# A gated feed-forward layer in split fp32: high-weight products cut into 362, 362 and 364 columns over three PSUM banks in place of four of 272

## The reference, cut to what matters

```python
def _swiglu(x, w_gate, w_up, w_down):
    return (jax.nn.silu(x @ w_gate) * (x @ w_up)) @ w_down

def _layer(x, state, p):
    f = _swiglu(_rmsnorm(x, p['ffn1_norm_pre']), p['ffn1_w_gate'], p['ffn1_w_up'], p['ffn1_w_down'])
    x = x + (0.5 * _rmsnorm(f, p['ffn1_norm_post'])).astype(x.dtype)
    m, new_state = _token_mixer(_rmsnorm(x, p['mix_norm_pre']), *state, p)
    x = x + _rmsnorm(m, p['mix_norm_post']).astype(x.dtype)
    f = _swiglu(_rmsnorm(x, p['ffn2_norm_pre']), p['ffn2_w_gate'], p['ffn2_w_up'], p['ffn2_w_down'])
    x = x + (0.5 * _rmsnorm(f, p['ffn2_norm_post'])).astype(x.dtype)
    return x, new_state
```

## Time and profile before

| | us |
|---|---|
| median of three runs | 3801.59 |
| lowest and highest | 3799.52, 3802.06 |
| the profiled execution, its own time | 3801.82 |
| its span, first to last instruction | 3799.8 |
| mean granted TensorE clock of the span | 0.932 |

### The profile page before, as it was taken

The page is one execution under the profiler, slowest core; times in us unless marked ns, Lnnn a source line. Parts: engine busy times, 40 slices in busy tenths (PEclk is TensorE's granted clock), DMA queues, the critical chain, the costliest instruction groups (busy, mean ns, idle before and its releaser), DMA issues. The chain is left out here.

```text
span 3799.8 us, 68663 instructions
## 1 busy us (share of the span) xinstructions
PE 3450.5 (91%) x25494; PEld 3262.0 (86%) x25494; DVE 1306.9 (34%) x1895; ACT 745.7 (20%) x1228; POOL 1556.6 (41%) x948
## 2 busy tenths in 40 slices
PE   8999899887877998999899998998778789989997
PEld 7999799866747997999889997998667479979997
DVE  2220275366444222221022202763564442132201
ACT  2110222223103112110021102322231021121100
POOL 4555466200004653555445553662000046535553
PEclk9999999999758999999999999999996589999999
DMA  3222122000103231222132222220001122312221
GB/s 120 88 85 84 55 90 86 28 0 0 63 23 100 88 93 56 86 88 84 51 93 88 87 83 61 84 88 20 0 0 63 57 75 88 92 56 88 87 83 64
DMA packets 77404, 258.82 MB, mean 68 GB/s; under 512 B 8272, under 2 KB 10064, under 8 KB 76496
## 3 DMA queue, kind: packets, MB, share of 16 engines
q1 hardware_dynamic: 76976, 256.43, 22.0%
q10 hardware_dynamic: 288, 0.49, 0.0%
HBM read 242.31 MB, written 14.58 MB: 68 GB/s over the span
## 5 line engine op out<-in xcount | busy, mean ns | idle before, releaser
L427 PE MATMUL ps<-hh,wh 128*128 128x272 f32 x4896 | 1422.3, 291 | 58.2 <-DVE hl L1255 45.0
L429 PE MATMUL ps<-hh,wl 128*128 128x272 f32 x4896 | 1419.0, 290 | 0.0
L428 PE MATMUL ps<-hl,wh 128*128 128x272 f32 x4896 | 1414.1, 289 | 0.0
L391 POOL TENSOR_SCALAR wh<-raw 128x1024 fp32r<-128x1024 f32 (+2 forms) x472 | 489.4, 1037 | 2141.8 <-PE ps L429 1220.9
L393 POOL TENSOR_TENSOR wl<-raw,wh 128x1024 fp32r<-128x1024 f32 (+2 forms) x472 | 1067.3, 2261 | 71.9 <-POOL wh L391 3.6
L427 PEld LDWEIGHTS ps<-hh,wh 128*128 128x128 f32 x4896 | 927.4, 189 | 69.5 <-issue 68.8
L428 PEld LDWEIGHTS ps<-hl,wh 128*128 128x128 f32 x4896 | 931.1, 190 | 0.0
L429 PEld LDWEIGHTS ps<-hh,wl 128*128 128x128 f32 x4896 | 928.3, 190 | 0.0
L427 PE MATMUL ps<-ah,wh 128*128 128x272 f32 x1408 | 410.2, 291 | 0.0
L429 PE MATMUL ps<-ah,wl 128*128 128x272 f32 x1408 | 405.8, 288 | 0.0
L428 PE MATMUL ps<-al,wh 128*128 128x272 f32 x1408 | 404.1, 287 | 0.0
(11 more groups left out here) (303 smaller groups left out, 3854.4 us busy)
## 6 DMA issues: line engine op xcount, KB each, us to landing
raw<-in_up SPq DMA_DIRECT2D x176, 512.0 KB, 3.6
raw<-in_win SPq DMA_DIRECT2D x80, 512.0 KB, 3.6
raw<-in_merge SPq DMA_DIRECT2D x96, 384.0 KB, 3.1
raw<-in_down SPq DMA_DIRECT2D x64, 512.0 KB, 3.5
raw<-in_down SPq DMA_DIRECT2D x32, 384.0 KB, 3.1
raw<-in_wout SPq DMA_DIRECT2D x16, 512.0 KB, 3.6
states<-in_in_gdn SPq DMA_DIRECT2D x2, 2048.0 KB, 8.3
proj<-in_in_ssd SPq DMA_DIRECT2D x2, 2048.0 KB, 15.7
```

Of the source, the lines that this page charges most:

```text
L391: pool.tensor_scalar(hi, src, 1.0, 1.0, MULT, MULT).then_inc(hi_done, 1)
L427: pe.matmul(out, wh[:, j % SPLIT, k, :], mh_[:, c], start=a, stop=False)
L428: pe.matmul(out, wh[:, j % SPLIT, k, :], ml_[:, c], start=False, stop=False)
L429: last = pe.matmul(out, wl[:, j % SPLIT, k, :], mh_[:, c], start=False, stop=b)
```

## The change

**Layout.** A k tile of the moving operand was two rows, high and low, of 544 each (hh and hl, ah and al). Now it is one row of 1,088 (hx, ax) with NEAR = 90, FAR = 182 and WIDE = 362: for each half [90 low columns, 272 high columns], and behind both halves [182 low, 182 low]. The high weights run over it in three matmuls, 362, 362 and 364 columns, into three banks (3 x slot, + 1, + 2); the low weights run over the 272 high columns of each half, onto columns 90 to 361 of the first two banks. Per k there are five matmuls in place of six, with the same number of columns.

**Joins.** The low columns' products now stand beside the high ones. `join` adds them with three reductions of VectorE over pairs of values that lie apart: 180 outputs (90 of each half) from the first two banks, then 182 of each half from its bank and the third one. A slot takes three banks, so there are two of them, and banks 6 and 7 are pair(3), into which VectorE writes the joined up product. The gate join goes to sil, where ScalarE applies Silu in place; in the down loop the join goes to f, and ScalarE squares f. ScalarE's copy L954 goes in the feed-forward stages.

**The rest.** `products`, which the mixer still uses, issues both halves of each of the three parts in turn. VectorE's low part is two instructions (180 and 364 columns). Some semaphores of the mixer are merged to make room for two new ones, with the same waits in number.

```diff
+        hx, ax = row("hx", 0, [P, KD, 2 * T], F32R), row("ax", 16, [P, KF, 2 * T], F32R)
...
+        def high_of(flat):
+            return flat[:, 0:2 * WIDE].rearrange("p (a t) -> p a t", a=2)[:, :, NEAR:WIDE]
...
+        def join(eng, slot, dst):
+
+            flat = ps[:, :, :].rearrange("p b c -> p (b c)")
+            near = ps[:, 3 * slot:3 * slot + 2, 0:2 * NEAR].rearrange("p a (e t) -> p a t e", e=2)
+            eng.reduce_sum(dst[:, :, 0:NEAR], near, axis=mybir.AxisListType.X)
+            for h in range(2):
+                a = (3 * slot + h) * 512 + 2 * NEAR
+                apart = (3 * slot + 2) * 512 + h * FAR - a
+                both_ = flat[:, a:a + 2 * apart].rearrange("p (e t) -> p t e", e=2)[:, 0:FAR, :]
+                last = eng.reduce_sum(dst[:, h, NEAR:HALF], both_, axis=mybir.AxisListType.X)
+            return last
...
+            def wide_product(layer, first, i, j, per, slot, nk, moving, start=True, stop=True, ready=None):
...
+                    def high():
+                        for h in range(2):
+                            pe.matmul(ps[:, 3 * slot + h, 0:WIDE], w, flat[:, h * WIDE:(h + 1) * WIDE], start=a, stop=b,
+                                      skip_group_check=True)
+                        return pe.matmul(ps[:, 3 * slot + 2, 0:2 * FAR], w, flat[:, 2 * WIDE:2 * T], start=a, stop=b,
+                                         skip_group_check=True)
+
+                    def low():
+                        for h in range(2):
+                            last = pe.matmul(ps[:, 3 * slot + h, NEAR:WIDE], wl[:, j % SPLIT, k, :],
+                                             flat[:, h * WIDE + NEAR:(h + 1) * WIDE], start=False, stop=False,
+                                             skip_group_check=True)
+                        return last
+
+                    for part in (high, low) if a else (low, high):
+                        last = part()
...
-                        pe.wait_ge(prod_done if j % 2 else sil_done, value(pe, layer * (2 * KF) + i * 2 + (which * KF + j // 2 + 1)))
-                        product(layer, first, i, j, 4, j, KD, h_tiles,
-                                ready=h_split(layer, 3 * which) if i is FIRST and j == 0 else None)
+                        pe.wait_ge(up_whole if j % 2 else gate_whole, value(pe, layer * (2 * KF) + i * 2 + (which * KF + j // 2 + 2)))
+                        wide_product(layer, first, i, j, 4, j % 2, KD, lambda k: hx[:, k, :],
+                                     ready=h_split(layer, 3 * which) if i is FIRST and j == 0 else None)
```

115 lines of the change are left out of this document (77 added, 38 removed).

## The result

The changed kernel takes **3809.2 us** (median of 14 runs, 3808.6 to 3811.0); the kernel before took 3800.7 us beside it (14 runs, 3798.8 to 3802.1). The ratio is 1.0024, with a 95% interval of 1.0017 to 1.0031: slower by 8.5 us, where 3783 and faster had been forecast. The profiled executions have spans of 3807.0 us (after) and 3799.8 us (before), so 7.2 us of the difference are to be found in the traces.

What follows compares the result with a forecast made beforehand. TensorE's matmul pace, 125.3 ns each, was taken to bound the feed-forward stages. From 3801.8 us, - 24.9 + 2.3 + 4.0 gave 3783.2, stated as 3783, with a range of 3735 to 3813.

Steps and rivals of the forecast that it cites:

- -24.9 (TensorE): Feed-forward products: one matmul of six goes in each of 2,112 k, at 12.0 ns each, 24.9 us saved.
- +2.3 (head): Head of each feed-forward stage: VectorE's low part takes 0.79 us against 0.72, adding 2.3 us, all on the path.
- 0 (up loop): Up loop, 88 pairs of gate and up blocks: joins of 1.43 us fit in VectorE's spare time, costing zero.
- +4.0 (tail): Tail of each feed-forward stage: join, hop and Square from SBUF end 1.0 us later, four times, 4.0 us.
- 0 (the rest): Other products, reordered with equal number and columns, ScalarE's high-part write and the merged semaphores: no cost or gain.
- nearest to that is a price per matmul: TensorE's matmuls at full clock: the 12.0 ns over the columns' time are paid once a matmul, whatever its width.
- rival 2: TensorE: the 12 ns grow with columns; time 3808 or 3801, block 6.01 us, 362-column pace 167 ns; 18%.
- In the down loop a join has 17 us: Down loop of the feed-forward stages: each join has 17 us of time, so no cost was put there.
- rival 3: Up loop: VectorE becomes the bound and TensorE waits for the gate join; 44 us more, 3827; 6%.
- if the pace of the untouched projection matmuls moved with their new order: Projection matmuls, reordered only: a moved pace would show the forecast wrong; no size was given.
- Rival 1: TensorE: the overhead hides behind wider matmuls, 80 us less, 3728, or in part anything up to 3783; 18%.
- Rival 4: Moving operands that no longer start at multiples of 1,088 bytes cost; 6 ns each give 3834; 6%.

Runs made afterwards that it cites:

- the run with the cut alone: Kernel before, with feed-forward matmuls of 362, 362, 364, 272 and 272 columns a k into its two banks, nothing joined: 3795.4 us against 3800.1, ratio 0.9987.
- the first sweep: Kernel before, with up-loop blocks of 512, 128, 400 and 200 columns in place of 272: 233.9 ns a matmul at 512 columns, 183.7 at 400.
- The run with the old order: Changed kernel, with the matmuls of the mixer's products in the order of before: 3812.8 us, ratio 1.0033 to the kernel before.

## Why the prediction was wrong, point by point

**The sum, term by term.** Predicted: -24.9 (TensorE), +2.3 (head), 0 (up loop), +4.0 (tail), 0 (the rest). Measured in the traces, four stages: cut -3.3 (from the run with the cut alone), head +2.0, rest of the up and down loops +1.3, **turn +7.3**, tail +5.5, mixer -3.4, norms -2.1. They add up to +7.3 against 7.2 in the spans. The first is the cut with its order, and the last two are of the size by which untouched parts differ between traces.

**The step that failed** is "nearest to that is a price per matmul". I had the paces of one width only (272 columns) and two facts beside it, nothing added at 1.2 GHz and 3 ns added with two passes; both fit a cost per column as well as one per matmul, and the text says so under rival 2. From one width no slope can be had. The sweep gives 2.2 ns a matmul and 0.036 ns for each column over the ideal; the matmul saved is worth some 2.2 ns and not 12.0, and the term of 24.9 us is 4.6 by that line and 3.3, the order included, in the stages' traces. The column's price hangs on the moving operand, as the repeated column shows (115.9 ns); that twice the time per column hides it is what the two facts say, and no run took them further.

I also set aside the rule of the Trainium skill (TensorE: Matmul & The Clock Gate, Back-to-back issue gap) wrongly. It has N/2.4 + 2.5 ns, and I compared its *level* with the trace, 115.8 against 125.3. For the change only its *step* mattered, 2.5 ns for a matmul less, 5.3 us. The constant of the first sweep's line, 2.2 ns (2.5 without the edges of the blocks), bears the step out; the run with the cut alone can't, since it changed the order too. The level holds for the repeated column (115.9) and for dense bf16 (116), and not for different fp32 columns.

**The turn was missed.** The part on the tail follows the last square to the end of the stage, and the same square has to be waited for at the end of the first half of the down loop. Before, it lay under the sums of the tile ahead and left hardly a trace. The change made it the last to end, 1.82 us four times. "In the down loop a join has 17 us" is true of six of the eight joins of a stage; the two at the ends of the halves, on which TensorE's own next step waits, have none.

**The tail** had the right mechanism and was mis-sized, 1.38 in place of 1.0: VectorE's first reduction starts 0.55 us after the last product does, where ScalarE's square started after 0.38, and the square starts 0.19 after the join, where 0.1 was put. A last 0.1 comes from the sums: "The squares' four matmuls (0.92 us) end before that table load does" no longer holds. They run from 440.26 to 441.42, the table load ends at 441.41, and ScalarE's next instruction starts 0.1 us after both, where before it followed the table load at once.

**The head** was right, 2.0 against 2.3: the low parts come every 1.40 us in place of 1.34. The timeline of VectorE in the first head (the earlier trace rows has the pattern of before):

```profile
27.80 0.53 DVE L1320 TENSOR_TENSOR hx<-hf,hx 128x364 fp32r<-128x364 f32 x1
...
29.20 0.53 DVE L1320 TENSOR_TENSOR hx<-hf,hx 128x364 fp32r<-128x364 f32 x1
...
30.60 0.53 DVE L1320 TENSOR_TENSOR hx<-hf,hx 128x364 fp32r<-128x364 f32 x1
```

**The up loop** at zero was nearly right, and the join at 1.43 us exactly. TensorE never waits for a joined bank, so rival 3 stays out. A block is 6.007 us long, 0.007 more than in the run with the cut alone; over the stage that is 0.3 us, whose cause, the third bank, VectorE's added traffic or the low weights going first, wasn't tried apart.

**"Nothing for the rest"** was wrong in the other direction. I named it as a sign ("if the pace of the untouched projection matmuls moved with their new order") and gave it no price: it moved. The run with the old order puts it at some 3.6 us, in line with the -3.4 between the traces' mixers.

**The rivals.** Rival 2 is what happened: blocks of 6.007 (sign: 6.01), 362-column matmuls at 166 ns from start to start (sign: 167), and a time of 3808 or 3801. That its 3808 is so near to 3809.2 is half luck: 8.8 us missed at the turn and the tail stand against 5.5 gained in the mixer and the norms. Rival 1 (overhead hidden) would have needed an excess that falls with the width; it grows, from 12.0 ns at 272 columns to 20.6 at 512. Rival 4: the starts cost nothing that a run showed, since windows that all start at column 0 run no faster. The range of 3735 to 3813 held the time; the chance of 0.70 for faster rested on the one step above.

## What to carry to other kernels

To forecast what another cut of the same work saves, get the pace at two widths before you price a matmul: an excess over the ideal pace at one width says nothing of whether it is paid per matmul or per column. When an eviction is handed from one engine to two in a row, look for each place where the producer itself waits for the last result, at the end of every inner half too, and not only at the end of the stage. And price a reordering even where counts and columns stay; here it gave more (-0.6%) than the change that was the subject cost.

## What the runs showed of the hardware that I had not expected

- Matmuls on fp32r with 128-column weights, three in a row into one bank, take 2.2 ns plus 0.4525 ns a column from 272 to 512 columns, and about 111 ns at 128 and at 200 columns. One repeated column (115.9 ns for 272) or bf16 values side by side (116) come within 3 ns of the 113.3 of their columns; bf16 values four bytes apart take 121.9.
- Matmuls of 272 columns that change the bank each time are cheaper by 0.8 ns each than three in a row into the same bank (124.4 against 125.3), whether the weights change at two or at five of six matmuls. This did not carry over to the mix of 362, 364 and 272 columns.
- 352, 352 and 384 columns cost 0.03 us more a block of 40 than 362, 362 and 364.
- fp32r and bf16 by turns in one accumulation: 382 ns for a group of three whose separate paces sum to 369.
- VectorE's reductions of 364 values from PSUM to 182 take 525 to 536 ns, a join of three 1.43 us in a row, with GpSimd at work beside them: what 153 ns and 1.04 ns a value give, with no surcharge for PSUM or for GpSimd.
